# Weight sums of a block-product FFN made in DRAM during the gate stage, and the transfers of the passes put in another order

## The reference, cut to what matters

```
def swiglu(x, w_in, w_out):
    gate, up = jnp.split(x @ w_in, 2, axis=-1)
    return (jax.nn.silu(gate) * up) @ w_out
...
y = h + 0.5 * rmsnorm(swiglu(rmsnorm(h, p['ffn2_pre']), p['ffn2_w_in'], p['ffn2_w_out']), p['ffn2_post'])
```

## Time and profile before

| | us |
|---|---|
| median of 3 runs | 3405.16 |
| lowest, highest | 3403.32, 3408.3 |
| profiled execution | 3413.99 |
| its span | 3412.4 |
| PE busy in the span | 3297.4 |
| DVE, ACT, POOL busy | 1892.9, 1464.0, 784.2 |

### The profile page before, as it was taken

One profiled execution on the slowest core, in us unless ns is written; L12 is line 12 of the kernel. 1 busy time (PEld: TensorE's weight loads), 2 busy tenths in 40 slices (PEclk: granted clock), 3 DMA queues, 4 the chain that ended last, 5 costly groups with the idle time before them and its releaser, 6 DMA issues. The chain is left out here.

```text
span 3412.4 us, 70726 instructions
## 1 busy us (share of the span) xinstructions
PE 3297.4 (97%) x28058; PEld 3127.3 (92%) x28058; DVE 1892.9 (55%) x3303; ACT 1464.0 (43%) x3030; POOL 784.2 (23%) x750
## 2 busy tenths in 40 slices
PE   7999999998999999999999999999999999998998
PEld 7999999997888888878899999998999899998987
DVE  6655565764555555544455555454442855555764
ACT  5222234555555455443444444344323622223554
POOL 3323310102222121000022222222001444452031
PEclk9999999999999999999999999899999999999999
DMA  4222237732222222389412221114522466666674
GB/s 167 76 79 81 86 114 224 226 126 81 69 70 69 70 70 69 109 286 375 157 53 59 59 59 59 47 59 134 169 78 83 137 156 157 154 151 194 204 251 147
DMA packets 377239, 427.52 MB, mean 125 GB/s; under 512 B 25304, under 2 KB 273192, under 8 KB 376766
## 3 DMA queue, kind: packets, MB, share of 16 engines
q1 hardware_dynamic: 355670, 372.37, 34.5%
q0 software_dynamic: 21168, 50.35, 6.1%
q10 hardware_dynamic: 84, 0.35, 0.0%
HBM read 343.08 MB, written 105.85 MB: 132 GB/s over the span
## 5 line engine op out<-in xcount | busy, mean ns | idle before, releaser
L673 PE MATMUL ps<-p_hi,w_hi 128*128 128x352 f32 x912 | 304.5, 334 | 3.0 <-PEq L123 1.4
L2062 PE MATMUL ps<-p_hi,w_hi 128*128 128x352 f32 x840 | 293.9, 350 | 3.2 <-issue 1.8
L673 PE MATMUL ps<-p_hi,w_lo 128*128 128x352 f32 x912 | 293.3, 322 | 0.0
L673 PE MATMUL ps<-p_lo,w_hi 128*128 128x352 f32 x912 | 293.0, 321 | 0.0
L2062 PE MATMUL ps<-p_lo,w_hi 128*128 128x352 f32 x840 | 280.2, 334 | 0.0
L2062 PE MATMUL ps<-p_hi,w_lo 128*128 128x352 f32 x840 | 279.9, 333 | 0.0
L673 PEld LDWEIGHTS ps<-p_hi,w_hi 128*128 128x128 f32 x912 | 172.1, 189 | 5.1 <-issue 1.9
L3418 PE MATMUL ps<-f_hid_hi,w_hi 128*128 128x352 f32 x528 | 171.3, 324 | 1.4 <-DVE w_lo L2581 1.3
L673 PEld LDWEIGHTS ps<-p_lo,w_hi 128*128 128x128 f32 x912 | 172.4, 189 | 0.0
L673 PEld LDWEIGHTS ps<-p_hi,w_lo 128*128 128x128 f32 x912 | 171.5, 188 | 0.0
L2062 PEld LDWEIGHTS ps<-p_hi,w_hi 128*128 128x128 f32 x840 | 162.3, 193 | 9.0 <-issue 3.8
(11 more groups left out here) (737 smaller groups left out, 10671.3 us busy)
## 6 DMA issues: line engine op xcount, KB each, us to landing
w_raw<-in_w_in_dram SPq DMA_DIRECT2D x67, 512.0 KB, 4.2
w_raw<-in_ffn_w_out_dram SPq DMA_DIRECT2D x123, 256.0 KB, 3.5
sa_v<-in_cache_v_dram SPq DMA_DIRECT2D x120, 256.0 KB, 6.5
w_raw<-in_ffn_w_in_dram SPq DMA_DIRECT2D x48, 512.0 KB, 5.1
sa_k<-in_cache_k_dram SPq DMA_DIRECT2D x72, 256.0 KB, 5.4
f_s<-in_ffn_w_out_dram SPq DMA_DIRECT2D x64, 256.0 KB, 3.6
pair_s<-in_ffn_w_out_dram SPq DMA_DIRECT2D x55, 256.0 KB, 4.1
d_hid<-f_gb SPq DMA_DIRECT2D x44, 264.0 KB, 2.1
```

What stands on the lines that cost most here:

```text
L673: mm = nc.tensor.matmul(m.ps[:, bank, 0:CH], a[:, k, w], b[:, f, cols(c)], start=(f == 0 and i == 0), stop=(f == KT - 1 and i == 2))
L2062: mm = nc.tensor.matmul(m.ps[:, (k + c) % 2, 0:CH], a[:, k, f * P:(f + 1) * P], x[:, f, cols(c)], start=(j == 0), stop=(j == len(terms) - 1))
```

## The change

1. Passes 4 and 6 too get their weight differences from DRAM. In steps 3 to 13 of the gate stage two tiles per step are loaded into one SBUF buffer (`pair_neg`), negated by ACT, stored to `d_w_sums` and there added to by a DMA of POOL. The subtractions of DVE and the second loads go. 33 sums become 55.
2. The last three tiles of pass 0's operand are loaded as two and one, at v = 0 and 1 instead of 3; the last of their sums takes its addend from SBUF and not from the stored copy. The loads of the other passes start up to five slots earlier or one later, and the operands of a pass are waited for in three groups.
3. The last chunk's 22 tiles come in six loads, and DVE makes their low parts, 14 of them in pass 6 and 8 in the first slots of h = 7. POOL makes only the sums of squares.
4. The residual of chunk 1 is loaded in slot (6,7) and not (7,0); the first scaled pairs stand at (5,8) to (6,1) and not (5,9) to (6,3).

The core of the diff:

```diff
+    NEGATED = {4: ((1, 1), (1, 0)), 6: ((0, 0), (0, 1))}
...
+    def flips_of(t):
+        return range(2 * (t - 3), 2 * (t - 2)) if 3 <= t < 3 + KH else range(0)
+
+    def flip_pairs(sp, t):
+        for n in flips_of(t):
+            p, k = FLIPS[n]
+            if n == 0:
+                sp.wait_ge(e.up_mm, 12 + 1)
+            else:
+                sp.wait_ge(e.neg_out, 16 * n)
+            sp.dma_start(neg, wout_tile(k, *NEGATED[p][0])).then_inc(e.neg_in, 16)
+            sp.wait_ge(e.neg_done, n + 1)
+            sp.dma_start(d_w[SUMS[p], k], neg).then_inc(e.neg_out, 16)
+
+    def flip(act, n):
+        act.wait_ge(e.neg_in, 16 * (n + 1))
+        nc.scalar.mul(neg, neg, -1.0).then_inc(e.neg_done, 1)
+
+    def add_flipped(pool, t):
+        for n in flips_of(t):
+            p, k = FLIPS[n]
+            pool.wait_ge(e.neg_out, 16 * (n + 1))
+            pool.dma_start(d_w[SUMS[p], k], wout_tile(k, *NEGATED[p][1]), accum_op=ALU.add).then_inc(e.w_added, 16)
...
-        pool.wait_ge(e.h_out[0], 16 * (s + 1))
+        if s == FT - 1:
+            pool.wait_ge(e.h_done, 6 + 2 * (FT - 3) + 1)
+        else:
+            pool.wait_ge(e.h_out[0], 16 * (s + 1))
...
+    def load_last_parts(sp, lo, hi):
+        sp.wait_ge(e.up_mm, 12 + N1)
+        sp.wait_ge(e.added[0], 16 * hi)
+        sp.dma_start(FIRST[2][:, lo - 8:hi - 8, :], d_first[lo:hi].rearrange("k p n -> p k n")).then_inc(e.first_in[2], 16)
...
-    def w_sum(dve, v):
-        r = RAW_OF[v]
-        raw_there(dve, r)
-        raw_there(dve, r + 1)
-        nc.vector.tensor_tensor(unit_raw(r), unit_raw(r), unit_raw(r + 1), ALU.subtract).then_inc(e.w_sum, 1)
...
+    def rest_low(dve, n):
+        dve.wait_ge(e.rest_hi, n + 1)
+        nc.vector.tensor_tensor(rest_tile(hid_lo, n), rest_value(n), rest_tile(hid_hi, n).bitcast(F32), ALU.subtract).then_inc(e.rest_lo, 1)
+
+    REST_AT = {2: (0,), 3: (1,), 4: (2, 3), 5: (4,), 6: (5, 6), 7: (7, 8), 8: (9, 10), 9: (11, 12), 10: (13,)}
...
             copy_pairs(sp, t)
+            flip_pairs(sp, t)
             store_h(sp, t, 0)
...
                 if quads:
+                    if i in (2, 5) and flips_of(t):
+                        flip(act, flips_of(t)[i // 3])
...
-                pairs = {(5, 9): (0, 0), (5, 10): (0, 1), (6, 1): (0, 2), (6, 3): (0, 3), (7, 10): (1, 0), (7, 11): (1, 1), (7, 12): (1, 2), (7, 13): (1, 3)}
-                sums_of = {(6, 4): (0, 0), (6, 5): (0, 1), (7, 14): (1, 0), (7, 15): (1, 1)}
+                pairs = {(5, 8): (0, 0), (5, 9): (0, 1), (5, 10): (0, 2), (6, 1): (0, 3), (7, 10): (1, 0), (7, 11): (1, 1), (7, 12): (1, 2), (7, 13): (1, 3)}
+                sums_of = {(6, 3): (0, 0), (6, 5): (0, 1), (7, 14): (1, 0), (7, 15): (1, 1)}
```

More of the change, by code:

```diff
@@ L2664, in raw_there @@
-    def raw_there(eng, r):
-        eng.wait_ge(e.out_full[r % 8], 16 * (r // 8 + 1))
+        else:
+            sp.wait_ge(e.out_lo, v - 7)
+        p, k = divmod(v, KH)
+        if v >= NQ:
+            half, k = divmod(v - NQ, FT)
+            src = wout_tile(k, 0, half)
+        elif p in PLAIN_W:
+            src = wout_tile(k, *PLAIN_W[p])
+        else:
+            if k == 0:
+                sp.wait_ge(e.w_added, 16 * (len(COPIES) + len(FLIPS)))
+            src = d_w[SUMS[p], k]
+        sp.dma_start(unit_raw(v), src).then_inc(e.out_full[v % 8], 16)
@@ L2676, in add_pairs @@
             a, half = PAIRED[p][1]
-            pool.dma_start(d_w[p - 1, k], wout[:, k + KH * a, half * 512:half * 512 + 512], accum_op=ALU.add).then_inc(e.w_added, 16)
+            pool.dma_start(d_w[SUMS[p], k], wout_tile(k, a, half), accum_op=ALU.add).then_inc(e.w_added, 16)
     def hid_part(s, b):
@@ L2699, in add_stored @@
         wait(pool, e.added[0], 16 * j)
-        pool.dma_start(d_first[j], hid_part(s, 0), accum_op=ALU.add).then_inc(e.added[0], 16)
+        pool.dma_start(d_first[j], hid_part(s, 0) if s < FT - 1 else hid[:, 0:W3], accum_op=ALU.add).then_inc(e.added[0], 16)
         pool.wait_ge(e.h_out[1], 16 * (s + 1))
@@ L2745, in x_high @@
         if p == 0:
-            act.wait_ge(e.first_in[g], 16)
+            act.wait_ge(e.first_in[g], 32 if g == 2 else 16)
         elif p == 3:
@@ L2778, in w_high @@
     def w_high(act, v):
[L2779 to L2782, removed]
+        raw_there(act, v)
         if v < 4:
@@ L2899, in quad_sync @@
         store_h(sp, FT - 1, 1)
-        r = 8
-        def raws(v):
-            nonlocal r
-            while r < len(RAWS) and RAWS[r][0] <= v:
-                load_raw(sp, r)
-                r += 1
         for v in range(NQ):
             p, k = divmod(v, KH)
-            raws(v + 6 if p else v + 8)
+            load_raw(sp, v + 8)
             if v == 0:
+                load_last_parts(sp, 8, 10)
                 for n in range(4):
@@ L2958, in quad_scalar @@
                     x_high(act, p + 1, k // 2 - 1)
-                elif p == 6 and k >= 2:
-                    rest_high(act, k - 2)
+                elif p == 6:
+                    for n in REST_AT.get(k, ()):
+                        rest_high(act, n)
             during(p, k)
@@ L2966, in quad_scalar @@
                     w_high(act, v + 3)
-                if h == 0 and 9 + k < FT:
-                    rest_high(act, 9 + k)
+                if h == 0 and 14 + k < FT:
+                    rest_high(act, 14 + k)
                 if h == 1 and k == 0:
@@ L3002, in quad_vector @@
                     x_sum(dve, 2)
+                if p == 6:
+                    for n in REST_AT.get(k, ()):
+                        rest_low(dve, n)
             during(p, k)
@@ L3008, in quad_vector @@
                     w_low(dve, v + 3)
+                if h == 0 and 14 + k < FT:
+                    rest_low(dve, 14 + k)
                 if h == 0 and k == 0:
@@ L3355, in gpsimd @@
             add_lower(pool, FT - 1)
[L3356 to L3357 removed]
+            add_rows()
+            sum_pool(pool, 1)
     def product(pe, t, i):
```

170 lines of the change are left out of this document (75 added, 95 removed).

## The result

The changed kernel took 3417.82 us (median of 7 runs, 3409.01 to 3428.34), the kernel before 3406.28 us beside it (3403.32 to 3414.97, 7 runs). The ratio is 1.0035, 95% interval 1.0021 to 1.0049: slower by 12 us, where 12 us of gain were forecast. The range held the time; the sign was wrong.

What follows compares the result with a forecast made beforehand. PE was taken as the bound, busy 97% of 3412.4 us, so only its stops could be won. Passes -21 and gate stage +9 gave -12: 3402 us for the profiled execution, 3393 against the median; range 3377 to 3419.

Steps and rivals of the forecast that it cites:

- the loop: Gate stage: two pair_neg tiles through one buffer per step, half 1 of hid to the next; 21.7 us against 20.4.
- the release of PE by DVE: Gate stage: PE stops ahead of a step's second product until DVE frees a bank, only from about the fourth flip step.
- the lossless lag of 5.1 us: Gate stage: bank free at 2877.3, wanted by PE at 2882.4, so 5.1 us of lag cost nothing.
- load one: Gate stage: a step's first pair_neg load, landed 9.1 us after half 1 of hid is ready, plus 0.6 for company.
- the store: Gate stage: store of the first negated tile to DRAM, 2.1 us alone, plus 1.1 beside one add, 3.2.
- load two: Gate stage: a step's second pair_neg load into the same buffer, 2.5 us alone, plus 1.1; upper bound 5.3.
- the tail of the loop: Gate stage: second flip 0.6, one high part 0.6, then 3.4 us from the SiLU's start to the next half 1.
- the second rival: Gate stage: the flip chain becomes the bound; at L = 24, 36 us lost, 19 won, 3422 us; chance 21%.
- The first tile: Pass 0: first-operand tiles 8 to 10 loaded earlier, so PE's wait for op_hid_lo shrinks; gain 10 us, bounds 6 to 11.5.
- The subtractions: Passes 4 and 6: DVE's 22 subtractions and 22 loads go, relieving slot (6,7); gain 6 us, bounds 3 and 8.
- the wait left at (6,7): Pass 6: PE's transposes ready at 3290.0, DVE's residual add at 3292.8, so a wait of 2.5 us stays.
- The last chunk: Last chunk: six rest loads, DVE splits, earlier residual, so weights are no longer issued late; gain 5 us, bounds 2 and 6.

Runs made afterwards that it cites:

- late tiles: Kernel with the first pair_neg load moved ahead, its last three first-operand tiles loaded as three at v = 3 again; 3392.94 us, ratio 0.9965 to before.
- spread: Changed kernel with the 22 negated tiles spread over steps 2 to 20, one a step, two in 6, 12 and 18; 3393.50 us, ratio 0.9964 to before.
- both cures: Changed kernel, first pair_neg load ahead of the w_in loads, negated tiles one a step, two in 6, 12, 18; 3381.79 us, second time 3381.55.

## Why the prediction was wrong

**The gate stage: the mechanism was right, a term of the loop was too small.** The loop, its place (the second flip ahead of the SiLU), the release of PE by DVE from about the fourth step on (the first stop is at 2792.6, in the third step with flips, when half 1 was 5.1 us late) and the lossless lag of 5.1 us stood in the prediction. Its length did not: 21.7 chosen, 23.8 measured, bounds 18.9 and 26.5. The step that failed is "I take +0.6 for load one (its add began before it), +1.1 for the store and for load two: L = 21.7". Load one needed +2.7 over the 9.1, the store +2.2; load two only +0.5, and the tail of the loop was 0.5 shorter than 4.6. Nearly all of load one's excess was there before it was issued: SyncE was through its copies 3.5 us after half 1 before, and 6.1 after it in the changed kernel. By the prediction's own formula, 11 x (23.8 - 20.4) - 5.1 gives 32 us; measured were 34.1, with 3.4 us at the lower clock after each of four of the sixteen stops. So the second rival came true: L = 24 and 36 us were its numbers. I gave it 21%, because I took the one row of a store beside one add (3.2) as nearest, though the same text says that two older adds fall on that store, and priced no delay of SyncE's own issues. A row for the older copies in a full queue (5.3), which I had as the upper bound for one term, was the nearer one for the crowded half of the step. One path was not in the prediction at all: it counted the add of each flipped tile as a transfer, not as a wait in GpSimd's order ahead of the sums of weights. In the changed kernel two of the sixteen stops come by it, and once the first load stands ahead of the copies, three of the four that are left.

**The passes: right in place, too small in two sizes.** 10 + 6 + 5 = 21 was forecast, with a bound of 25; 27.8 were measured. The first tile: forecast 10, by the run with late tiles 8.7. The subtractions: forecast 6 (3 to 8), measured 9.7 by the profiles and 5.8 by the medians; the wait left at (6,7) is 0.8 and not 2.5, and small gaps in pass 4 went too. The last chunk: forecast 5 (2 to 6), measured 5.9 by undoing loads, splits and residual. These add up to 24.3; the remaining 3.5 us are not assigned (the profiles of kernels with equal passes differ by up to 2).

**The cause that I named for the last chunk is not enough.** "The SP queue (SyncE) waited there for POOL's splits": with the splits on GpSimd and each single load waiting for them, but the residual early, the passes take 262.9 and PE stops there for no more than 1.9 us. In these runs the 8 to 9 us of the late transfers come only with the residual ahead of them; the wait for a split is then one short link (0.8 us) between two slow loads. The wait for the row copy at (7,11), 2 us forecast, is there with 1.9.

**What stays open.** The net of the profiles is +6 us, that of the medians +12: the profiled execution of after is one of the faster. Several kernels with flips scatter by 14 to 19 us between runs (changed 3409 to 3428, spread 3387 to 3401, late tiles 3385 to 3401, both cures 3377 to 3391 the second time), the one without flips by 7 and others with flips by 3; the kernel before, run beside them, by 5 to 15, so the scatter is not the flips' alone. With one profile of each, where a slower run loses its time is not shown.

## What to carry to other kernels

Work that an idle engine has time for can still cost a whole stage, if it is one link in a loop of transfers through in-order queues: write the loop down from one iteration to the next, and price each transfer with what is released in the same microsecond, not as alone, and ask of every engine that waits for a link what stands behind that wait in its own order (here ScalarE's high parts and GpSimd's sums). Put the head of such a loop first in its queue and one link per iteration; here that turned +12 us into -19 to -24 (ratios 0.9945 and 0.9928) with the same bytes. For a stop behind a late transfer, look for the largest transfer issued just ahead of it before blaming the wait in front of it.

## What the runs showed of the hardware

- A DMA share of 0.82 and 199 GB/s left PE full in one order; 0.83 and 199 cost 9% of the stretch in another, and 0.88 and 220 in a third only 2.5%.
- The issue of DMAs on SyncE took longer with more in flight: two copies of 256 KB took 1.95 us to issue in a step before, 4.21 in one with the added traffic.
- A 256 KB store from SBUF to DRAM: 2.1 us alone, 4.3 beside two adding transfers of the same size, 5.9 in the mean beside copies and w_in loads.
- A 144 KB load issued 1.3 us after one of 1.5 MB landed after 8.4 us; with the big one elsewhere such loads took 3.8.
